# Attention heads in pairs whose score matmuls alternate between the two halves of the array, and a norm cut into 16 pieces

## The reference, cut to what matters

```python
# x: (512, 1024); per layer
h = rms_norm(x)
proj = h @ w_in                    # queries, keys, values of four mixers, and 4 x 1024 gate columns
o_a = neighborhood_attention(...)  # A: 4 heads of 64, local window on a 64-wide grid, bias per offset
o_b = window_sink_attention(...)   # B: 4 heads of 64 on 2 key heads, |i - j| <= 128, sink logit
o_c = dense_block_attention(axial_rope(rms_norm(cq)), axial_rope(rms_norm(ck)), cv)   # C: 4 on 2, dense
o_d = dense_block_attention(...)   # D: 4 heads of 96, dense
y = sum_b sigmoid(gate_b) * (o_b @ w_branch_b)
x = x + rms_norm(y @ w_out)
x = x + rms_norm(swiglu(rms_norm(x)))
# a head: p = softmax(q @ k.T * scale + bias);  o = p @ v
```

## Time and profile before

| | us |
|---|---|
| median of the runs | 1899.0 |
| the profiled execution, its time | 1897.93 |
| the profiled execution, its span | 1896.1 |
| PE busy in the span | 1769.1 |
| DVE busy | 928.5 |
| POOL busy | 1132.1 |
| ACT busy | 410.6 |

### The profile page before, as it was taken

The page is one execution under the profiler, slowest core; times in us unless marked ns, Lnnn a source line. Parts: engine busy times, 40 slices in busy tenths (PEclk is TensorE's granted clock), DMA queues, the critical chain, the costliest instruction groups (busy, mean ns, idle before and its releaser), DMA issues.

```text
span 1896.1 us, 21091 instructions
## 1 busy us (share of the span) xinstructions
PE 1769.1 (93%) x8162; PEld 1426.5 (75%) x8162; DVE 928.5 (49%) x1621; ACT 410.6 (22%) x875; POOL 1132.1 (60%) x1172
## 2 busy tenths in 40 slices
PE   7999999799979999999789999998999799999996
PEld 6778778577667888888677787776676678888885
DVE  5754653865646333310277546458655553343002
ACT  3441312233222111100134313123232311111000
POOL 6537455334466788777574363643435668787774
PEclk9999999999989999999899999998999899999998
DMA  5114111111121222222231141211111212222231
GB/s 215 67 45 111 67 67 67 67 45 48 64 90 45 106 95 89 97 88 96 74 120 67 47 131 45 82 75 45 45 67 48 85 67 89 93 108 77 91 106 60
DMA packets 25779, 151.34 MB, mean 80 GB/s; under 512 B 2955, under 2 KB 4235, under 8 KB 11824
## 3 DMA queue, kind: packets, MB, share of 16 engines
q1 hardware_dynamic: 22176, 141.21, 20.9%
q10 hardware_dynamic: 3504, 8.78, 1.6%
HBM read 147.88 MB, written 4.70 MB: 80 GB/s over the span
## 4 chain that ended last, share of the span: by engine, by line
PE 83%; DVE 12%; issue 2%; ACT 2%; POOL 1%; DMA 0%; ACTq 0%; DVEq 0%
PE main L609 15%; PE main L505 11%; PE main L506 11%; PE main L507 11%; PE work L505 10%; PE work L506 9%; PE work L507 9%; PE turn L674 2%; PE pv L505 2%; PE pv L506 1%; PE pv L507 1%; DVE tiny L1171 1%; DVE yt L1340 1%; DVE h_lo L1145 1%; DVE tiny L1173 1%
## 5 line engine op out<-in xcount | busy, mean ns | idle before, releaser
L447 POOL TENSOR_SCALAR w_hi<-raw 128x512 fp32r<-128x512 f32 (+3 forms) x576 | 380.4, 669 | 706.9 <-issue 684.5
L451 POOL TENSOR_TENSOR w_lo<-raw,w_hi 128x512 fp32r<-128x512 f32 (+3 forms) x576 | 749.7, 1312 | 0.0
L609 PE MATMUL main<-h_hi,w_hi 128*128 128x512 f32 x512 | 216.8, 423 | 0.0
L609 PE MATMUL main<-h_lo,w_hi 128*128 128x512 f32 x512 | 211.0, 412 | 0.0
L609 PE MATMUL main<-h_hi,w_lo 128*128 128x512 f32 x512 | 209.3, 409 | 0.0
L505 PE MATMUL main<-h_hi,w_hi 128*128 128x512 f32 x480 | 192.6, 401 | 16.4 <-DVE h_lo L1145 15.7
L506 PE MATMUL main<-h_lo,w_hi 128*128 128x512 f32 x480 | 190.4, 397 | 0.0
L507 PE MATMUL main<-h_hi,w_lo 128*128 128x512 f32 x480 | 190.1, 396 | 0.0
L505 PE MATMUL work<-h_hi,w_hi 128*128 128x512 f32 x480 | 188.6, 393 | 0.0
L506 PE MATMUL work<-h_lo,w_hi 128*128 128x512 f32 x480 | 188.1, 392 | 0.0
L507 PE MATMUL work<-h_hi,w_lo 128*128 128x512 f32 x480 | 188.0, 392 | 0.0
(11 more groups left out here) (196 smaller groups left out, 3011.8 us busy)
## 6 DMA issues: line engine op xcount, KB each, us to landing
raw<-stream SPq DMA_DIRECT2D x106, 1024.0 KB, 4.8
raw<-stream SPq DMA_DIRECT2D x32, 704.0 KB, 4.1
raw<-stream SPq DMA_DIRECT2D x4, 832.0 KB, 5.0
x<-x_in ACTq DMA_DIRECT2D x4, 512.0 KB, 9.1
t_line<-t_first ACTq DMA_DIRECT2D x2, 1024.0 KB
rpb<-rpb_line ACTq DMA_DIRECT2D x16, 128.0 KB, 7.4
out<-x SPq DMA_DIRECT2D x8, 256.0 KB, 2.2
bias_b<-t_line ACTq DMA_DIRECT2D x2, 768.0 KB, 5.1
```

The lines of the kernel that those rows point to most:

```text
L447: pool.tensor_scalar(w_hi[:, slot, parts[q]], raw[:, slot, parts[q]], 1.0, 0.0, ALU.mult, ALU.add).then_inc(piece_hi, 1)
L451: e = pool.tensor_tensor(w_lo[:, slot, part], raw[:, slot, part], w_hi[:, slot, part].bitcast(F32), ALU.subtract)
L609: mm = pe.matmul(main[m % 2][:, :], w, (h_lo if which == 1 else h_hi)[:, k, :], start=(s % STEPS == 0), stop=(s % STEPS == STEPS - 1))
```

## The change

- The heads of A, B and C are taken two at a time (`head_pair`). In the score phase both heads' score for a block of queries are done together, six matmuls in the order even, odd, even, odd, even, odd, into two of the three banks; then gate steps follow. TensorE waits for both banks before the first of the six.
- The turn phase has eight steps, four of the even head and four of the odd. Values of a step follow the transposes and gates of the next.
- The odd head's probabilities have places of their own (`odd_a`, `odd_b`, `odd_c`). To make room, keys of B and C move to `kb_hi`, `kb_lo`, and the offsets for A's bias are held for two heads at a time, loaded by eight DMAs of half the size twice in a layer; the second eight stand in ACT's queue ahead of A's first exponential.
- A's biases for heads 2 and 3 are built in the turn phase of the first pair, behind steps 4 and 6.
- C's norm and rotation are cut into 16 slices (`c_slice`), one behind the low part of each of the 16 turn steps of B.
- The gate matmuls are spread anew; their number per mixer stays 192. In C, gates are scaled after t = 1 and t = 3.
- D is unchanged.

```diff
+SCORES = {b: [(h, t) for h in range(4) for t in range(NT)] if b == "D" else
+          [(2 * j + i, t) for j in range(2) for t in range(NT) for i in range(2)] for b in BR}
-    WORK += [("score", _b, h, t) for h in range(4) for t in range(NT)]
+    WORK += [("score", _b, h, t) for h, t in SCORES[_b]]
...
-    heads, last = dict(D=((4, 4, 4, 11, 4, 3, 2, 4, 0), (4, 4, 3, 8, 4, 2, 2, 3, 4)),
-                       A=((7, 7, 7, 7, 2, 2, 2, 2, 0), (6, 6, 6, 6, 2, 2, 1, 1, 6)),
-                       B=((9, 9, 9, 9, 3, 3, 3, 3, 0), (8, 8, 8, 8, 3, 3, 2, 2, 6)),
-                       C=((5, 5, 5, 13, 6, 5, 4, 5, 0), (5, 5, 5, 11, 5, 5, 3, 5, 4)))[b]
+    spread = dict(D=3 * (4, 4, 4, 11, 4, 3, 2, 4, 0) + (4, 4, 3, 8, 4, 2, 2, 3, 4),
+                  A=(7, 7, 7, 22, 5, 5, 3, 2, 3, 2, 3, 2, 4) + (7, 7, 7, 16, 4, 4, 2, 2, 2, 2, 2, 2, 15),
+                  B=(8, 8, 8, 20, 6, 6, 6, 6, 6, 6, 6, 6, 4) + (8, 8, 8, 20, 6, 6, 6, 6, 6, 6, 6, 6, 4),
+                  C=(9, 9, 9, 28, 6, 6, 4, 4, 4, 4, 4, 4, 5) + (9, 9, 9, 24, 5, 5, 3, 3, 3, 3, 3, 3, 17))[b]
-    for n in 3 * heads + last:
+    for n in spread:
...
-    return len(GATE_BEFORE[b]) + 9 * h + n
+    return len(GATE_BEFORE[b]) + (9 * h + n if b == "D" else 13 * (h // 2) + n)
+
+
+def score_number(b, h, t):
+
+    return 16 * BR.index(b) + SCORES[b].index((h, t))
...
+    if b == "C":
+        return {1: (0, 1), 3: (2, 3)}.get(t, ())
...
+    odd_a = sb("odd_a", [P, 1280], F32, QT + 15 * K)
+    odd_b = sb("odd_b", [P, 1280], F32, KT + 4 * K)
+    odd_c = sb("odd_c", [P, NT, S], F32, QT + 8 * K)
...
-                    q = 16 * BR.index(n[1]) + 4 * n[2] + n[3]
-                    pe.wait_ge(max_done if banded(n[1]) else exp_done, at(l, 64, q + 1))
+                    pe.wait_ge(max_done if banded(n[1]) else exp_done, at(l, 64, score_number(*n[1:]) + 1))
...
+            def head_pair(l, b, j):
+
+                even, odd = 2 * j, 2 * j + 1
+                (qe_h, qe_l), (ke_h, ke_l) = queries(b, even), keys(b, even)
+                (qo_h, qo_l), (ko_h, ko_l) = queries(b, odd), keys(b, odd)
+                for t in range(NT):
+                    we, wo = WORK_AT[("score", b, even, t)], WORK_AT[("score", b, odd, t)]
+                    ks, rows = window(b, t), slice(P * t, P * t + P)
+                    cols = slice(P * ks[0], P * (ks[-1] + 1))
+                    n = P * len(ks)
+                    wait_work(l, we)
+                    wait_work(l, wo)
+                    e, o = work[we % 3][:, 0:n], work[wo % 3][:, 0:n]
+                    pe.matmul(e, qe_h[:, rows], ke_h[:, cols], start=True, stop=False)
+                    pe.matmul(o, qo_h[:, rows], ko_h[:, cols], start=True, stop=False)
+                    pe.matmul(e, qe_h[:, rows], ke_l[:, cols], start=False, stop=False)
+                    pe.matmul(o, qo_h[:, rows], ko_l[:, cols], start=False, stop=False)
+                    pe.matmul(e, qe_l[:, rows], ke_h[:, cols], start=False, stop=True).then_inc(work_done, 1)
+                    pe.matmul(o, qo_l[:, rows], ko_h[:, cols], start=False, stop=True).then_inc(work_done, 1)
+                    gate_steps(l, b, gate_point(b, even, t))
+                tiles = [(h, k) for h in (even, odd) for k in range(NT)]
+                for i, (h, k) in enumerate(tiles):
+                    turn_prob(l, b, h, k)
+                    gate_steps(l, b, gate_point(b, even, 4 + i))
+                    if i:
+                        values(l, b, *tiles[i - 1])
+                values(l, b, odd, NT - 1)
+                gate_steps(l, b, gate_point(b, even, 12))
 
             def branch_out(l, b):
...
+            def head_pair(l, b, j):
+
+                even, odd = 2 * j, 2 * j + 1
+                for t in range(NT):
+                    exponent(l, b, even, t)
+                    exponent(l, b, odd, t)
+                    for n in gates_after(b, t):
+                        gate_tanh(l, b, gate_point(b, even, n))
+                for i in range(2 * NT):
+                    prob_high(l, b, even + i // NT, i % NT)
+                    gate_tanh(l, b, gate_point(b, even, 4 + i))
+                output_high(l, b, j)
+                gate_tanh(l, b, gate_point(b, even, 12))
...
+                act.wait_ge(bias_built, at(l, 4, 2))
+                load_offsets(1)
+                for j in range(2):
+                    head_pair(l, "A", j)
...
+            def c_slice(l, i):
+
+                if i == 0:
+                    dve.wait_ge(copied, at(l, N_COPY, COPY_AT["Ckv1"] + 1))
+                    c_squares(l, 0, 4)
+                elif i == 1:
+                    c_sums(l, 4)
+                elif i == 2:
+                    c_root(l, 16 // NT)
+                elif i == 3:
+                    c_scale(l, 0, 4)
+                elif i == 4:
+                    c_gain(l, 0, 4, "cq")
+                elif i == 5:
+                    c_squares(l, 4, 2)
+                    c_sums(l, 2)
+                elif i == 6:
+                    c_root(l, 2)
+                    c_scale(l, 4, 2)
+                elif i == 7:
+                    c_gain(l, 4, 2, "ck")
+                else:
+                    g0, n = (0, 4) if i < 12 else (4, 2)
+                    f = (i - 8) // 2 % 2
+                    if i % 2 == 0:
+                        c_products(l, g0, n, f)
+                    else:
+                        c_turned(l, g0, n, f)
 
             def window_bias(l, h):
...
-                    src = view(rpb[:, h, 16 * b0:], [[16, nb], [RPB_ROW, ROWS], [1, 16]])
+                    src = view(rpb[:, h % 2, 16 * b0:], [[16, nb], [RPB_ROW, ROWS], [1, 16]])
...
+            def head_pair(l, b, j):
+
+                even, odd = 2 * j, 2 * j + 1
+                for t in range(NT):
+                    maximum(l, b, even, t)
+                    maximum(l, b, odd, t)
+                    if t:
+                        normalise(l, b, even, t - 1)
+                        normalise(l, b, odd, t - 1)
+                    if t == NT - 1:
+                        normalise(l, b, even, t)
+                        normalise(l, b, odd, t)
+                    for n in gates_after(b, t):
+                        gate_scale(l, b, gate_point(b, even, n))
+                for i in range(2 * NT):
+                    prob_low(l, b, even + i // NT, i % NT)
+                    if b == "A" and j == 0 and i in (4, 6):
+                        if i == 4:
+                            dve.wait_ge(rpb_in_place, 256 * l + 256)
+                        window_bias(l, 2 + (i - 4) // 2)
...
+                        c_slice(l, 2 * NT * j + i)
+                    gate_scale(l, b, gate_point(b, even, 4 + i))
+                output_low(l, b, j)
+                gate_scale(l, b, gate_point(b, even, 12))
```

More of the change, by code:

```diff
@@ L311, in program @@
     ident, mean = c("ident"), c("mean")
-    negmax, sums, recip, esink, maxima = (tiny[:, 4 * i:4 * i + 4] for i in range(5))
+    negmax, sums, recip, esink, maxima = (tiny[:, 8 * i + 76:8 * i + 84] for i in range(5))
     r_in, r_out, r_tmp = tiny[:, 0:24], tiny[:, 24:48], tiny[:, 48:72]
@@ L677, in values @@
-                def values(k):
-                    if h == 0 and k == 0:
-                        wait_split(l, ("V", b, NT - 1))
-                    qs = [q for q in range(NT) if k in window(b, q)]
-                    a, z = P * qs[0], P * (qs[-1] + 1)
-                    wait_split(l, ("prob", b, h, k))
-                    v = slice(HD * (h % 2), HD * (h % 2) + P)
-                    j = "BC".index(b) if b in "BC" else h // 2
-                    mm = three(pv[:, a:z], v_hi[:, k, j, v], v_lo[:, k, j, v], pt_hi[:, k % 2, a:z],
-                               pt_lo[:, k % 2, a:z], h % 2 == 0 and k == 0, h % 2 == 1 and k == NT - 1, skip_group_check=True)
-                    if h % 2 == 1 and k == NT - 1:
-                        mm.then_inc(pv_done, 1)
@@ L804, in _ @@
                 by_token(l, "Ckv1", PIECE["Ckv"], (2, 3), 0, 256, 256)
-                for h in range(4):
-                    if h == 0:
-                        wait_split(l, "Bk")
-                    head(l, "B", h)
+                wait_split(l, "Bk")
+                for j in range(2):
+                    head_pair(l, "B", j)
                 for j in range(3):
@@ L812, in _ @@
                 branch_out(l, "B")
-                for h in range(4):
-                    if h == 0:
-                        wait_split(l, ("C", 2))
-                    head(l, "C", h)
+                wait_split(l, ("C", 2))
+                for j in range(2):
+                    head_pair(l, "C", j)
                 branch_out(l, "C")
@@ L1098, in _ @@
                     else:
-                        hi(l, ("C", j), ka_hi[:, 0, :], src)
-                for h in range(4):
-                    head(l, "C", h)
+                        hi(l, ("C", j), kb_hi[:, :], src)
+                for j in range(2):
+                    head_pair(l, "C", j)
                 for d in range(KD):
```

(18 more changed lines are left out.)

283 lines of the change are left out of this document (155 added, 128 removed).

## The result

The changed kernel takes 1852.7 us (median of 4 runs, 1851.6 to 1854.2) against 1898.7 for the one before: ratio 0.975, 95% interval 0.974 to 0.976. I had forecast 1851. The sum is right, two of its terms are not: they are off by some 10 us each, in opposite directions, and that they cancel is luck.

A forecast was written before the change was run, and what follows sets the result against it. The chain was taken to run through PE, busy 1769 of 1896 us. Terms -19.7 - 15.7 - 16.2 + 1.7 + 2.0 = -47.9 us took 1897.9 to 1850.0, predicted median 1851 us; 8 in 10 range 1832 to 1876.

The forecast's parts named there:

- Visits: PE's score groups: visits to 64 rows fall from 96 to 48, each saving 0.41 us, -19.7 us.
- Overlap: Six score matmuls of a group: an even and an odd one run at once, -15.7 us.
- only the loads of the weights stay in series: Within a score group matmuls of the two halves overlap, but their weight loads follow 0.11 us apart.
- C's norm in slices: In B: 33.2 us of waiting before scores goes, about 17 comes back in the turn phase, -16.2 us.
- The queue that I ran: DVE's slices in B's turn phase, run through with traced durations: 8.6 us of PE waits a layer.
- No single wait reaches the 4.90 of today, so I expect the clock to stay high: In B, with sliced work, PE's waits stay shorter than before, so the granted clock does not drop.
- that is one maximum on DVE under 7 or 8 gates: free: In A and B, getting the even bank back before the next score group costs PE nothing.
- DVE binds B: Rival: slices beside POOL delay every second low part, the 33 us stay; 1867 to 1873 us, chance 0.16.
- A, +1.7: A's biases for heads 2 and 3 move into the turn phase: net 0.85 us a layer, +1.7 in all.
- Two banks at a time in C: C's score groups: PE waits 0.5 us for banks in each of four pairs, +2 us (bounds 0 and +8).
- The series: Rival: in score groups the halves do not run at once; 1866 us, chance 0.20.
- the drain rivals: Rival: every change of half costs like a change between 64 and 128 rows; 1916 us, chance 0.07.

The follow-up runs named there:

- experiment 2: Changed kernel with half of a block's gates between the even head's three score matmuls and the odd head's three: 1900.6 us (0.9998).
- experiments 3 and 4: 3: changed kernel, all six score matmuls of a group in the same 64 rows, 1863.4 us. 4: same edit on a further edited version (1831.9), 1854.0 us.
- experiment 5: Changed kernel with C's norm and rotation left out, the slices issuing no vector operations: 1832.3 us (0.964).

## Why the prediction was right, point by point

**Visits, -19.7.** Right in the distances: 0.42 us each, 20 us. No run prices them alone in time; experiment 2 has waits of its own.

**Overlap, -15.7.** The term was mis-sized. The step "only the loads of the weights stay in series" failed: the earlier trace rows show two loads for the same 128 rows, and I carried them over to loads for different halves. Out of PE's work it takes 25.4 us, the upper of the two numbers that stood in the text. Its worth in this kernel is 10.7 us, since 15 come back as waits and lower clock (experiments 3 and 4). So 15.7 was too little as work and too much as time.

**C's norm in slices, -16.2.** Counting waits of B and of C's transposes, -7.1 us was measured (-2.9 - 5.4 + 1.2). The queue that I ran had the right places: the first root (I said 1.7 us, it is 1.94), the second root with its scaling, the four products (1.8 forecast, 2.17 measured). Two steps failed. "No single wait reaches the 4.90 of today, so I expect the clock to stay high": in layer one it falls behind waits of 1.9 and 2.2 us, though in layer two it stays up behind the same ones; the falls cost some 1.6 us. And "that is one maximum on DVE under 7 or 8 gates: free" left out a wait ahead of each pair's fourth group, 1.13 us at 311.16, which is not there when the overlap is taken away (experiment 3). The rival "DVE binds B" was half true: C's work holds 20 us (experiment 5), where my text had 33 before and 17 after. Nor was all of the 33 us waiting: in B and C's transposes PE's waits are 25.4 us before and 22.1 after, and the clock is low for 27.3 us before and 10.2 after. Of the 7.1 us some 3 are waits, and the rest goes with the clock; no run takes the two apart.

**A, +1.7.** +5.4 measured. The waits behind the biases are 1.22 and 0.29 us a layer, where I had 0.7 and 1.4. Missing were waits of 0.35 and 0.75 us ahead of scores, the second behind the two normalisations beside POOL (1.20 and 1.19 us, 0.35 where POOL is idle). The one gate tile that I had left in, with its tanh ahead of a high part, costs 1.68 us in the second pair and not 0.85. The DMA issues cost nothing.

**Two banks at a time in C, +2.0.** +1.6: right in size. The trace has a single wait for ACT in it, 0.33 us in layer two; what makes up the rest stays open. The same wait is dearer in A and B, where I had written "free".

**Sum.** -20 - 25 + 5 - 7 + 2 = -45 and -46 measured; mine was -47.9. As work the overlap was put 10 us too low and the slices brought 9 us less than I had; that these cancel is luck, while the visits were right. The series and the drain rivals fall by the first timeline: the gaps stand only at a group's ends.

What stays open: why the clock falls behind a wait of 1.94 us in one layer and not behind the same wait in the other.

## What to carry to other kernels

Two 64-row matmul streams in different halves of the array run at once if they are in PE's queue together (they wrote different banks in every run here); their order doesn't matter, but the gain is only as large as the slack of the engine that hands the banks back, so look at that engine before counting it. Work cut into slices must be cut by its cost beside POOL, not by its cost alone, and by what a step of PE's covers: the same sixteen slices lost 18.5 us in short steps, gained 27 over one block in long ones, and the slices cut anew, with the two roots made one in three parts, another 13. A small operation of the kind shown beside POOL costs what is left of the POOL instruction under way, so the number of such operations counts, not only their length. After each repair of a wait read again what stands beside what: a faster PE moves POOL's work onto other operations.

## What the runs showed of the hardware

Matmuls and loads of different row halves start within 0.01 us of each other, out of queue order (the fourth ahead of the second). The granted clock fell to 1.2 GHz behind an idle time of 1.94 us in layer one, and did not behind 1.94 and 2.26 us in layer two. A small DVE operation that starts while POOL splits weights ended 0.01 to 0.04 us behind the POOL instruction under way, 116 times of 116. So a chain of eleven took 7.8 us with eight beside POOL, 4.4 with three beside it, and 2.17 (8 values, at 335.34) with POOL idle. Operations that read a bank took the same with and without POOL (0.40 to 0.43 us).
